# Attention's output product moved into the expert stage: 128 tokens first, 384 between the weighted sums

## The reference

```python
x = x + gate1 * (o @ w_o)                       # the product that is moved
h = rms_norm(x, norm2_g) * (1 + scale2) + shift2
qp = h @ w_pq                                   # 8 heads x 2 halves x 128
sc = einsum(qp, sub_keys)                       # 128 keys per half
# top 16 of each half, top 16 of their 256 sums: 16 experts a head and token, softmax gate g
a = einsum("d,kd->k", h, peer_u[experts])
y = einsum("k,kd->d", g * gelu(a), peer_v[experts])
out = x + gate2 * y
```

## Time and profile before

| | us |
|---|---|
| median of 3 runs (2904.01 to 2912.17) | 2907.8 |
| profiled execution | 2909.3 |
| its span | 2907.2 |
| PE busy | 2427.2 (83%) |
| DVE busy | 2107.1 (72%) |
| POOL busy | 1183.1 (41%) |
| ACT busy | 1005.5 (35%) |
| chain that ended last: DMA / PE / DVE | 20% / 13% / 7% |
| HBM read | 664.7 MB, of it 536.9 MB by gathers |

### The profile page before, as it was taken

How to read it: one execution, slowest core, us unless ns; L and a number is a source line. 1 busy time by engine, 2 the same in 40 slices (tenths; PEclk the granted TensorE clock), 3 DMA queues, 4 the chain that set the end, 5 groups by cost and what they waited for, 6 DMA issues and landing times. The chain is left out here.

```text
span 2907.2 us, 36383 instructions
## 1 busy us (share of the span) xinstructions
PE 2427.2 (83%) x12256; PEld 1686.2 (58%) x12256; DVE 2107.1 (72%) x4034; ACT 1005.5 (35%) x2031; POOL 1183.1 (41%) x972
## 2 busy tenths in 40 slices
PE   7998979999999999999987988866766666766665
PEld 7998979999999896555565433322222222222222
DVE  7466857777777886455555777788878888788876
ACT  3222245666666622344343222222222222221221
POOL 3453446666666430111122434434444444443442
PEclk9999989999999999999998999988888888888899
DMA  3332831222222164101015999999999999999998
GB/s 113 87 95 80 246 92 54 59 58 58 58 58 58 38 195 123 26 27 30 8 51 219 398 418 415 418 394 421 422 421 416 394 421 421 415 390 421 421 421 337
DMA packets 271501, 668.51 MB, mean 230 GB/s; under 512 B 13685, under 2 KB 203290, under 8 KB 205578
## 3 DMA queue, kind: packets, MB, share of 16 engines
q0 software_dynamic: 73952, 536.91, 44.7%
q1 hardware_dynamic: 196816, 129.73, 15.2%
q10 hardware_dynamic: 602, 0.24, 0.0%
HBM read 664.74 MB, written 2.10 MB: 229 GB/s over the span
## 5 line engine op out<-in xcount | busy, mean ns | idle before, releaser
L2468 PE MATMUL peer_py<-peer_uv,peer_diag 128*128 128x512 f32 x1536 | 835.6, 691 | 353.2 <-ACT peer_diag L2382 331.1
L2145 POOL DMA_INDIRECT peer_uv<-k_peer_uv,peer_idx x512 | 504.7, 986 | 776.9 <-PE peer_py L2468 725.4
L2468 PEld LDWEIGHTS peer_py<-peer_uv,peer_diag 128*128 128x128 f32 x1536 | 320.2, 221 | 829.8 <-issue 821.4
L2257 DVE SCALAR_TENSOR_TENSOR peer_spare<-peer_uv,peer_hp 128x1024 bf16<-128x1024 f32 x512 | 622.4, 1217 | 235.5 <-DMA peer_uv<-k_peer_uv,peer_idx 233.8
L1265 PE MATMUL hgrn_pp<-p_hx,p_whl 128*128 128x264 f32 x3024 | 394.1, 288 | 0.7 <-POOL p_whl L1118 0.7
L1265 PEld LDWEIGHTS hgrn_pp<-p_hx,p_whl 128*128 128x128 f32 x3024 | 377.0, 190 | 1.7 <-POOL p_whl L1118 1.1
L2374 ACT ACTIVATE peer_ga<-peer_a 128x2 f32<-128x2 f32 x256 | 52.0, 203 | 844.9 <-DVE peer_spare L2257 843.7
L1118 POOL TENSOR_TENSOR p_whl<-p2n_w,p_whl 128x1024 fp32r<-128x1024 f32 x62 | 147.9, 2396 | 205.3 <-ACT p_whl L1163 205.3
L772 PE MATMUL pool_ps<-p_raw,pool_wh 128*128 128x264 f32 x1024 | 172.0, 291 | 15.6 <-POOL pool_wl L899 10.3
L2382 ACT ACTIVATE peer_diag<-keep_ident,peer_wt 128x128 f32<-128x128 f32 x384 | 140.1, 396 | 115.3 <-DVE peer_wt L2266 112.6
L899 POOL TENSOR_TENSOR pool_wl<-pool_w,pool_wh 128x1024 fp32r<-128x1024 f32 (+1 forms) x48 | 103.0, 2148 | 155.0 <-ACT pool_wh L839 155.0
(11 more groups left out here) (434 smaller groups left out, 4245.7 us busy)
## 6 DMA issues: line engine op xcount, KB each, us to landing
p2n_w<-in_hgrn_w_in SPq DMA_DIRECT2D x62, 512.0 KB
pool_w<-in_pool_w_in SPq DMA_DIRECT2D x32, 512.0 KB
pool_out_aw<-in_w_ada SPq DMA_DIRECT2D x16, 768.0 KB, 4.8
hgrn_out_aw<-in_w_ada SPq DMA_DIRECT2D x16, 768.0 KB, 4.8
p_w<-in_w_pq SPq DMA_DIRECT2D x10, 1024.0 KB
peer_uv<-k_peer_uv,peer_idx POOLq DMA_INDIRECT x512
pool_out_w<-in_pool_w_out SPq DMA_DIRECT2D x7, 1024.0 KB, 7.7
p3a_wf<-in_w_in SPq DMA_DIRECT2D x12, 512.0 KB
```

The costliest lines, as they stand in the source:

```text
L2145: pool.indirect_dma_start(out=uv[:, n % DEPTH].rearrange("p w d -> p (w d)"), out_offset=None, in_=io["k_peer_uv"], in_offset=bass.Indirec ...
L2257: dve.scalar_tensor_tensor(out=spare[:, n % 2, :], in0=uv[:, n % DEPTH, 0, :], scalar=1.0, in1=hp[:, t % 2, :], op0=ALU.mult, op1=ALU.mult ...
L2468: last = pe.matmul(py[:, h * 512:(h + 1) * 512], diag[:, products(n) % DIAGS, :], uv[:, n % DEPTH, 1, h * 512:(h + 1) * 512], start=n % (P ...
```

## The change

- The product phase `attn_out` is gone. Its product is computed in `peer_phase` in plain fp32, not on split operands: `out_products(m, k, span)`. The whole `w_o` (4 MB) is loaded in the latent stage, behind that stage's small tables (`latent_behind`), into `wo`; what is free of it later holds the projections of three heads and the buffers `xtok`, `g2` and `rows`.
- First all 64 products for tokens 0 to 127 are run; DVE adds them to `xT` (`take_out`), ACT squares (`square`), TensorE sums each square's columns against ones (`column`), and the norm's root is taken of one column, inverted and spread again by TensorE (`spread_roots`).
- The 64 products for the other 384 tokens are put between as `fill(n)`: 5 single ones before `scores(1)`, 11 behind it, one in each slot of unit 0, two in each slot of unit 1. Their rows are taken by DVE before unit 0 (2) and by `EVACS` in units 0 to 2 (6); their norm is made in unit 2.
- Heads 0 to 5 are projected for 128 tokens first, and 4, 0, 1, 2, 3, 5 again for the other 384 in units 2 and 3 and 5 to 9; heads 6 and 7 at once for all. That takes 12 loads of `w_pq` and not 10, all but one from the seventh on through slot 0 (head 5 stays in slot 1).
- `turn_h(1)` moves from unit 0 to unit 6, `turn_x(0)` and the product that spreads the gate to unit 5. `xT` becomes a part of `hT`, and `h2` takes the place of `oT`; `weighted` lies in the latter's space.

```diff
+        own = ph.sb("qT", [P, PH - 3, 2, SEQ])
+        lent = [wo[:, h, :].rearrange("p (j t) -> p j t", j=2) for h in range(3)]
+        qT = [own[:, n] for n in range(PH - 3)] + lent
...
+        xtok, g2, rows = wo[:, 5:7, :], wo[:, 7, :], wo[:, 3:5, :]
...
+        parts = [(n, None, FIRST) for n in range(6)] + \
+            [(n, j, span) for n, span in ((4, REST), (6, WHOLE), (7, WHOLE), (0, REST), (1, REST), (2, REST), (3, REST),
+                                          (5, REST)) for j in range(2)]
         part_at = {e: i for i, e in enumerate(parts)}
+        loads = [(0, 0), (1, 1), (2, 0), (3, 1), (4, 0), (5, 1), (6, 0), (7, 0), (0, 0), (1, 0), (2, 0), (3, 0)]
+        frees = {2: (0, None, FIRST), 3: (1, None, FIRST), 4: (2, None, FIRST), 5: (3, None, FIRST), 6: (4, 1, REST),
+                 7: (6, 1, WHOLE), 8: (7, 1, WHOLE), 9: (0, 1, REST), 10: (1, 1, REST), 11: (2, 1, REST)}
+        WITHIN = {(0, 1): (2, None, FIRST), (0, 7): (3, None, FIRST), (1, 5): (4, None, FIRST), (2, 4): (5, None, FIRST),
+                  (2, 13): (4, 0, REST), (3, 0): (4, 1, REST), (3, 7): (6, 0, WHOLE), (3, 10): (6, 1, WHOLE)}
+        TAKEN = {(0, 1): (2, None, FIRST), (0, 5): (3, None, FIRST), (1, 4): (4, None, FIRST), (2, 3): (5, None, FIRST),
+                 (3, 0): (4, 0, REST), (3, 1): (4, 1, REST), (3, 5): (6, 0, WHOLE), (3, 6): (6, 1, WHOLE)}
+        for i, (n, span) in enumerate(((7, WHOLE), (0, REST), (1, REST), (2, REST), (3, REST), (5, REST))):
+            WITHIN.update({(4 + i, 2): (n, 0, span), (4 + i, 6): (n, 1, span)})
+            TAKEN.update({(4 + i, 3): (n, 0, span), (4 + i, 5): (n, 1, span)})
+        EVACS = {(0, 12): 2, (1, 4): 3, (1, 8): 4, (1, 12): 5, (2, 0): 6, (2, 3): 7}
+        h2 = keep["oT"]
+        pair = [hp[:, 1, 0:SEQ], hp[:, 1, SEQ:]]
...
+            def take_out(m, span):
+                a, b = span
+                dve.wait_ge(o_summed, m + 1 + (KC if span == REST else 0))
+                x = xT[:, m, a:b]
+                dve.scalar_tensor_tensor(out=x, in0=pair[m % 2][:, 0:b - a], scalar=mod[:, 2 * KC + m:2 * KC + m + 1],
+                                         in1=x, op0=ALU.mult, op1=ALU.add).then_inc(o_taken, 1)
...
+            for m in range(KC):
+                take_out(m, FIRST)
+            add_columns(FIRST)
+            invert(FIRST)
+            for c in range(KC):
+                scale(c, FIRST)
             dve.wait_ge(k_in, 16)
             note(dve.tensor_copy(place[:, :, :], count[:, :].rearrange("p (a k) -> p a k", k=1)
                                  .to_broadcast([P, TOPK, TOPK])))
@@ -2301,9 +2361,10 @@
                 for piece in range(11):
                     route(r, piece)
                 if r == 0:
+                    take_out(0, REST)
                     keys(0, 0)
                     keys(0, 1)
-                    norm.dve(dve, 1)
+                    take_out(1, REST)
             inverse(0)
...
+                    if (s, k) in EVACS:
+                        take_out(EVACS[s, k], REST)
+                    if s == 2 and k == 6:
+                        add_columns(REST)
+                    if s == 2 and k == 7:
+                        invert(REST)
+                    if s == 2 and 9 <= k < 13:
+                        scale(2 * (k - 9), REST)
+                        scale(2 * (k - 9) + 1, REST)
...
+            act.activation(warm[:, :], keep["eps"][:, 0:1], ACT.Sqrt)
+            for m in range(KC):
+                square(m, FIRST)
+            root(FIRST)
+            for c in range(KC):
+                shift(c, FIRST)
             take_q(0, None, FIRST)
             take_c(0)
-            act.wait_ge(x_turned, 1)
-            act.activation(g2[:, :], py[:, :], ACT.Copy).then_inc(x_taken, 1)
             take_q(1, None, FIRST)
             take_c(1)
-            take_x(0)
             exps(0)
-            norm.shifts(act, 1)
+            square(0, REST)
+            square(1, REST)
             exps(1)
...
+                    for (u, k), m in EVACS.items():
+                        if (s, at) == (u, k // 2):
+                            square(m, REST)
+                    if s == 2 and at == 2:
+                        root(REST)
+                    if s == 2 and at >= 5:
+                        for c in {5: (0, 1), 6: (2, 3, 4, 5), 7: (6, 7)}[at]:
+                            shift(c, REST)
+                    if s == 5 and at == 6:
+                        act.wait_ge(x_turned, 1)
+                        act.activation(g2, hp[:, 1, :], ACT.Copy).then_inc(x_taken, 1)
+                    if s == 6 and at == 0:
+                        take_x(0)
...
+            def out_products(m, k, span):
+                a, b = span
+                if k == 0 and (m >= 2 or span == REST):
+                    pe.wait_ge(o_taken, m - 1 + (KC if span == REST else 0))
+                last = pe.matmul(pair[m % 2][:, 0:b - a], wo[:, k, m * P:(m + 1) * P], h2[:, k, a:b],
+                                 start=k == 0, stop=k == KC - 1)
+                if k == KC - 1:
+                    last.then_inc(o_summed, 1)
+            def column(m, span):
+                pe.wait_ge(sq_done, m + 1 + (KC if span == REST else 0))
+                for j in range(1 if span == FIRST else TT - 1):
+                    x = SEQ - P + j * (KC // 2) + m // 2
+                    to = pQ[:, m:m + 1] if span == FIRST else pair[m % 2][:, x:x + 1]
+                    last = pe.matmul(to, sq[:, j * P:(j + 1) * P], keep["ones"][:, 0:1], start=True, stop=True)
+                if m == KC - 1:
+                    last.then_inc(n_summed, 1)
+            def spread_roots(span):
+                pe.wait_ge(inverted, 1 if span == FIRST else 2)
+                for j in range(1 if span == FIRST else TT - 1):
+                    to, r = (pC[:, 0:P], 0) if span == FIRST else (pair[1][:, j * P:(j + 1) * P], 1 + j)
+                    last = pe.matmul(to, roots[:, r:r + 1].to_broadcast([P, P]), ident[:, :], start=True, stop=True)
+                last.then_inc(spread, 1)
+            placed = [0]
+            def fill(n):
+                for i in range(placed[0], placed[0] + n):
+                    m, k = divmod(i, KC)
+                    if k == KC - 1 and m:
+                        column(m - 1, REST)
+                    out_products(m, k, REST)
+                placed[0] += n
...
+            pe.wait_ge(wo_in, 16)
+            for m in range(KC):
+                for k in range(KC):
+                    if k == KC - 1 and m:
+                        column(m - 1, FIRST)
+                    out_products(m, k, FIRST)
+            fill(1)
+            column(KC - 1, FIRST)
+            fill(1)
+            spread_roots(FIRST)
+            fill(1)
             project(0, None, FIRST)
+            fill(1)
             scores(0)
             turn_h(0)
-            for c in range(KC):
-                last = pe.matmul(py[:, c * P:(c + 1) * P], mod[:, 5 * KC + c:5 * KC + c + 1].to_broadcast([P, P]),
-                                 ident[:, :], start=True, stop=True)
-            last.then_inc(x_turned, 1)
             project(1, None, FIRST)
+            fill(1)
             scores(1)
-            pe.wait_ge(x_taken, 1)
-            turn_x(0)
-            project(2, 0, WHOLE)
-            pe.wait_ge(x_taken, 2)
+            fill(11)
...
+                    if (s, k) in WITHIN:
+                        project(*WITHIN[s, k])
                     if s == 0 and k == 4:
                         scores(2)
-                    if s == 0 and k in (6, 9):
-                        project(3, 0 if k == 6 else 1, WHOLE)
-                    if s and k in (2, 6) and s + 3 < PH + 2:
-                        project((s + 3) % PH, 0 if k == 2 else 1, WHOLE if s + 3 < PH else REST)
-                    if k == (12 if s else 13) and s + 3 < UNITS:
+                    if s < 2:
+                        fill(1 + s)
+                    if s == 2 and k == 3:
+                        column(KC - 1, REST)
+                    if s == 2 and k == 6:
+                        spread_roots(REST)
+                    if s == 5 and k == 9:
+                        for c in range(KC):
+                            last = pe.matmul(hp[:, 1, c * P:(c + 1) * P],
+                                             mod[:, 5 * KC + c:5 * KC + c + 1].to_broadcast([P, P]), ident[:, :],
+                                             start=True, stop=True)
+                        last.then_inc(x_turned, 1)
+                    if s == 5 and k == 13:
+                        pe.wait_ge(x_taken, 1)
+                        turn_x(0)
+                    if k == (13 if s in (0, 3) else 12) and s + 3 < UNITS:
                         scores(s + 3)
-                    if s % PH == 0 and k == 8 and t + 1 < TT:
+                    if s == 6 and k == 10:
+                        pe.wait_ge(x_taken, 2)
+                        turn_h(1)
...
+            wo2 = ph34.sb("wo2", [P, KC, D])
...
```

(22 more changed lines are left out.)

149 lines of the change are left out of this document (82 added, 67 removed).

## The result

| | before | after |
|---|---|---|
| median | 2909.99 us (2904.01 to 2913.26, 4 runs) | 2889.24 us (2884.71 to 2895.25, 4 runs) |
| ratio | | 0.9932, 95% interval 0.9905 to 0.9960 |
| span of the profiled execution | 2907.2 us | 2892.9 us |
| end of attention (its last ACT instruction) | 1489.08 us | 1494.36 us |
| first gather | 1567.09 us | 1530.08 us |

The change makes the kernel faster, by 20.7 us. The forecast was 36.8 to 37; its sign is right and its size is not: the time lies just above the range. The last three rows of the table say where to look. From the end of attention to the first gather the kernel took 78.0 us and takes 35.7: 42.3 us gained, 39.8 forecast. The gather stage that follows is 22.7 us longer, 3 forecast. (The two profiled executions differ by only 14.3 us, because attention ended 5.3 us later in that of after.)

What follows compares the result with a forecast made beforehand. Kernel's end taken as first gather's time plus the gathers' own time plus queue idle time. -39.8 (first gather) -4 (opening) +5 (loads) +2 (unit 8) = -36.8, forecast 2871 us; range 2861 to 2889.

Steps and rivals of the forecast that it cites:

- Part 1: End of attention to first gather: product phase goes, 128 tokens come; first gather 39.8 us earlier, bounds 34 to 43.
- The 1.4 us for a cold start: Time added to the 128-token output products for TensorE starting at half clock after standing still at attention's end.
- Part 2: Opening of the gather stage: of 9.1 us lost today, 5 us stay lost; gain 4 us, between +7 and -3.
- the ring: Eight gather buffers, 19.9 us of transfers, said to cover unit 1's excess TensorE work and any wait for weights.
- Rival (a): Units 0 to 2: fillings let the queue run dry, ten hand-overs of 2.4 us paid in full; 2890 us, 12%.
- Rival (b): Units 0 to 3: fillings and waits hold TensorE at half clock, so the kernel is slower; 2922 at 80 us, 3%.
- Part 3: Gather stage: two more weight loads cost 5.0 us; head 6's load, the tightest, is hidden with 2 us to spare.
- 17.4 us later: Head 6's weights in unit 3: time from slot freed (slot 0) to needed (slot 7), against a load of at most 15 us.
- Part 4: Work moved late: projections in unit 8 behind a store cost 2 us, between 0 and 5; other moved work nothing.
- The late norm: Norm of the other 384 tokens on DVE and ACT: nothing under a full queue, or counted in the opening's 5 us.
- Rival (d): First gather waits for something unseen (output matrix, fillings), so the 40 us come back as waiting; 2905 us, 3%.

Runs made afterwards that it cites:

- fill27: Changed kernel with 16 fillings moved from unit 1 to TensorE's idle time before the first weighted sum (27 in a row, not 11): 2879.09 us, ratio 0.9903.
- nofill: Changed kernel with 7 of 8 products of each filling row left out from the third row on, all hand-overs kept: 2882.30 us, ratio 0.9898.
- evac: Changed kernel with DVE's rows of the filling products taken about two slots earlier, TensorE's work the same: 2886.26 us, ratio 0.9923.
- slot3: Changed kernel with head 6's weights loaded early into free output-matrix space, and head 7's load started when head 4 is projected: 2876.61 us, ratio 0.9887.
- both: Changed kernel with the edits of fill27 and slot3 together: 2869.98 us, ratio 0.9870.
- again: The changed kernel measured once more, nothing edited: 2886.79 us, ratio 0.9919.

## Why the forecast missed

**Part 1, the front, was right.** 42.3 us against 39.8, inside its bounds of 34 to 43. The 1.4 us for a cold start were not there: 30 instructions in 3.59 us are 0.12 each, the full clock, from the first on (granted 1.00 from 1495.35 to 1511.50), so the product was not cold even at its start, where the prediction had it cold. The first projection (4.23 us from 1514.84) ends 24.7 us after attention's end and the first gather is 11.0 us behind it; the forecast had 26.4 and 11.8. Rival (d) is out. Read from the first gather alone this looks worse (1530.08 against the 1527.3 forecast), since attention ended 5.3 us later in this execution; in the thirteen others profiled it ended between 1484.9 and 1492.0.

**Part 2, the opening, failed in a size and in the reason given for it.** I found unit 1's 48.3 us of TensorE work against 39.9 us of transfers and wrote that it "may borrow from the ring: eight buffers are 19.9 us". The unit took 53.6 us, 5.3 more than its work, by one late hand-over and the half clock behind it. And the ring lends less than its 19.9 us. The unit took 13.7 us more than its transfers, and 8.8 us were lost there, so an estimate from these two is that the ring lent some 5 us. The reason lies in the order of the kernel: gather n + 8 needs product n, and product n needs gather n to have landed and then DVE's dot product and ACT's gelu and diagonals, so part of the ring is always on that way. How large that part is no run measures. TensorE was not late when the unit began: it waited 0.94 us for the first diagonals, and DVE waited 1.46 us for a gather to land (until 1589.95). It fell behind within the unit. The place for the work was the 10.6 us of idle time ahead of the first product, as fill27 shows. Lost: 8.8 us in unit 1 alone, where I had 5 for units 0 to 3. Over the first 160 us after lost 6.5 us more than before, where the forecast had 4 less. Unit 0 went better than I had it (0.5 us lost in each window behind the first). Rival (a)'s time, 2890, nearly came true, but by luck: about half of the loss is the load's, and its mechanism, hand-overs paid in full, is the smaller part of unit 1's. nofill keeps each of them and has no hole there, and evac, which takes the wait away, has the same time. Rival (b) is out: over windows of 20 us the granted clock is 0.74 or more wherever it is shown, but for the first (0.66).

**Part 3, the loads.** Two more loads cost 5.0 us as forecast (5.5 and 4.9 measured). The step that failed is the next one: "17.4 us later ... so at most 15 us: hidden, with 2 us to spare; if not, TensorE waits and the ring (19.9 us) covers it". Each part of it failed. The bound of 15 us was twice the 7.6 us of half the size, but that is the store of `rows`, whose runs are 4 KB (by the rule above 3 x 1.25 us and a start of 3 to 4, so about 7.5); at 1 KB beside 8 KB gathers a load takes 25. The 17.4 us presumed a TensorE on its beat; late, it asked after 8.6. And the ring does not cover the wait, because the projection comes behind it: 8.35 + 9.49 us without a weighted sum in after, 8.38 + 10.18 in nofill, and windows of 317 and 237 GB/s. The stretch from 160 to 240 us behind the first gather lost 10.7 us more than before, where the forecast had nothing, and slot3 gives back 10.2 us in the median. The gap of head 7, just as short, the prediction did not look at.

**Part 4.** The stretch behind the first tile's store loses 4.9 us (352 and 390 GB/s at 1920 to 1960: 3.3 + 1.5) where before lost 4.8: nothing for the 2 us forecast. The output matrix's load and the turns cost nothing that shows. The late norm, which the forecast put at nothing, may cost a little: at the end of unit 2 TensorE waits 3.35 us for diagonals, with DVE busy throughout just before, and the 40 us behind unit 1 lose 2.7 us even in `both` where before lost 0.5. No run separates that.

**The sum again, in measured terms:** -42.3 (front) + 5.0 (loads) + 17.9 (lost transfer time more than before) = -19.4, and the medians differ by 20.7. Nearly all of the 17.9 lies in the first 240 us behind the first gather. Transfer time lost there, in us, from one profile each:

| run | 0 to 80 | 80 to 120 | 120 to 160 | 160 to 240 | sum | stage |
|---|---|---|---|---|---|---|
| before | 9.1 | 0.6 | 0.5 | 1.0 | 11.2 | 1340.1 |
| after | 3.8 | 8.9 | 4.0 | 11.7 | 28.5 | 1362.8 |
| again | 4.7 | 8.8 | 4.0 | 8.4 | 25.9 | 1360.7 |
| evac | 3.4 | 3.8 | 6.0 | 9.1 | 22.3 | 1355.2 |
| nofill | 3.5 | 2.0 | 5.7 | 13.3 | 24.5 | 1358.4 |
| slot3 | 3.7 | 7.8 | 2.7 | 4.9 | 19.1 | 1352.0 |
| fill27 | 3.4 | 0.9 | 5.4 | 4.3 | 14.0 | 1347.8 |
| both | 3.5 | 0.5 | 2.7 | 2.7 | 9.4 | 1342.5 |

The two repairs do not simply add: each alone takes some of the other's hole with it. By these profiles the fillings weigh more than the load, by the medians (7.7 and 10.2) less. What stays open: the exact share of each in a run, since TensorE's lateness sets which load waits (8.35, 4.2, and in fill27 2.1 us), and why attention's end scatters by some 9 us between executions.

## What to carry to other kernels

A buffer ring hides lateness only up to its depth less the way from arrival to release; before placing work "under the transfers", set each unit's work against its transfers, and put the excess where the engine is idle. A wait and the long work behind it count as one stop for the ring. Price a load beside a saturated gather queue by the ratio of run lengths, not by its bytes: its cost in queue time is its bytes (2.5 to 2.75 us for 1 MB with 1 KB runs here), but its landing is (1 + gather run / load run) times that and a start of 3 to 4 us, and each freed-to-needed gap must hold it. Mend all such gaps of one kind together, or the wait passes to the next.

## What the chip showed that I had not expected

- The same 1 MB on SP's queue landed in 5.5 us alone and, beside a full queue of 8 KB gathers, in 9.1, 11.3, 25.1 and 45.0 us with runs of 8 KB, 4 KB, 1 KB and 512 bytes; the time of the kernel did not follow (2872.99, 2873.41, 2869.98, 2871.74 us).
- The way from attention's end to the first gather repeats within 0.02 us over the thirteen profiled executions with this front (35.72 to 35.74), while attention's end itself lies between 1484.9 and 1494.4.
- How fast TensorE runs behind a short wait differs between executions of one and the same place. At the end of unit 2 it waits 3.35 or 3.36 us; the product behind it took 3.45 us in after, 2.69 in slot3 and 1.95 in both, where the full clock gives some 1.9 (rows of after's chain and of the timeline of both):

```profile
1671.23 3.45 PE peer_py L2614 x4
```

```profile
1658.57 1.95 PE L2622 MATMUL peer_py<-peer_uv,peer_diag 128*128 128x512 f32 x4 [3.36 <-ACT peer_diag L2481]
```
